# Turning roped rows one step later, and a new order of VectorE's and ScalarE's work at a head's end

## The chip, the cores and the metric

The kernel runs on one core of a Trainium2 chip. Four compute engines work side by side, each on its own list of instructions: TensorE (PE: matrix products and transposes, which write to PSUM), VectorE (DVE), ScalarE (ACT) and GpSimd (POOL). They wait for each other by semaphores. The metric is the device time of one execution in microseconds (us).

## The reference

One layer of an encoder, applied with the same weights to a prompt of 256 and a sample of 512 tokens of width 1024. In short:

```
h   = rms_norm(x)
p   = h @ w_in                         # q, k, v, gates, ... of all head groups
a   = gated linear attention (4 heads, chunks of 64, forward and backward scans summed)
d   = differential attention (4 heads, QK norm and rotary embedding)
x   = x + concat(a, d) @ w_out
x   = x + expert_choice_swiglu(rms_norm(x))   # 16 experts, each picks its own tokens
```

The change touches the place where `d`'s query and key columns are projected, normed and rotated while `a` is computed:

```
q = apply_rope(rms_norm(q, qn_g)) * (DIFF_DH ** -0.5)
k = apply_rope(rms_norm(k, kn_g))
scores = einsum('bhncd,bhnsd->bhncs', q * exp(b - b_mid), k * exp(b_mid - b))   # of the linear attention
```

## The kernel before

All 768 tokens are held as six tiles of 128. Every fp32 product is made of three: both operands are split into a high and a low part, and high x high, low x high and high x low are summed in PSUM. Weights are therefore split as they come: ScalarE writes the high part (`high_parts`, line 1017), VectorE the low part (`low_parts`, line 1375). The projection runs by slices of 512 columns of `w_in`; a slice has eight parts of 128 rows, and the buffer `wih` for high parts exists once, so the next slice's can only be written when the last product of the slice before is done.

The change lies in the head loop, 24 steps (`BODY = 4 * NT`), six to each of the four heads of the linear attention. Step i (head h = i // 6, tile t = i % 6) holds one projection unit on TensorE: 24 matmuls of 128x512 for tile t of the slice that belongs to head h. Heads 0 and 2 have the slices with the query and key columns of the differential attention (`dqk` units, "rotary" steps); heads 1 and 3 have slices that need only a copy (`tok` units). Around them, written out by hand, stands the rest:

- Rotary steps, for row number v: TensorE's product; ScalarE squares it (`squares`, line 1060); VectorE sums the squares (`sum_squares`, line 1470); ScalarE takes logarithm and exponential (`root_qk`, lines 1067 and 1068); VectorE refines them to inverse roots (`inverse_roots`, lines 1482 to 1484); ScalarE scales the rows from PSUM to `yr` (`rows_scaled`, line 1076), which frees the PSUM bank. One step later GpSimd multiplies the swapped halves (line 502), VectorE does the cosine half (`cosine_half`, line 1492) and the sum of both (`rope_add`, line 1476). TensorE turns the roped rows (a `rope` unit, line 644), two steps after their product, and ScalarE copies them out (line 1048).
- Linear attention of head h: `factors` (ScalarE's exponentials, lines 1097 to 1100, in step 3) for head h + 1; `score_factors` (VectorE, lines 1432 and 1433) multiplies them with queries and keys, and GpSimd multiplies the state keys (`state_factors`, line 514). TensorE makes `scores` (line 665) at the start of the head, VectorE masks them (`mask`, line 1443, for the prompt and for the sample), TensorE turns the keys (line 677) in the first step, does the updates (line 690) in the second and the outputs (lines 702 and 706) in the fourth.
- Last step of a head (t = 5, `turning`): high and low parts of the next slice.

Each engine takes its instructions in the order in which they are written. A unit takes the PSUM bank `u % 4`, u being its number in `tile_plan`, and waits until the unit u - 4 has been read out:

```python
if 4 <= u < len(UNITS) - 2:
    pe.wait_ge(*freed_count(u - 4))
```

`tile_plan` lists dqk, rope, gate and tok units in TensorE's order. Before, step 3 to 7 read: dqk(3), rope(1), dqk(4), rope(2), dqk(5), rope(3), tok(0), rope(4), tok(1), rope(5), where rope numbers are row numbers.

## Time and profile before

| | us |
|---|---|
| median of 3 runs | 1540.5 (1540.43 to 1540.51) |
| span of the profiled execution, first to last instruction | 1538.5 |
| TensorE busy | 1503.3 |
| VectorE busy | 1242.1 |
| ScalarE busy | 1090.5 |
| GpSimd busy | 141.4 |

The head loop takes from about 95 to 268 us of the span. The diff's other end, the expert layer, is three quarters of the whole and is not touched. Starts are counted from the span's first instruction. A duration of several pipelined instructions reaches a little past the start of the next one.

### The profile page before, as it was taken

The numbers are of one execution on the slowest core, as the hardware profiler recorded it, in microseconds if no ns is written. First come the engines' busy times: TensorE is split into PE (matmuls) and PEld (weight loads), VectorE is DVE, ScalarE is ACT, GpSimd is POOL, SyncE is SP. The second block draws the span as 40 slices with busy tenths as digits, with TensorE's granted clock in tenths as the row PEclk, the third lists the DMA queues.
The fourth block names the chain that finished last, engine by engine and source line by source line (L and its number), as shares of the span: only waits on it lengthen the run. The fifth ranks groups of instructions, "written<-read, shape, count | busy, mean of one in ns | idle before, by whom it ended". The sixth has DMA issues, their size and how long they took to land.

```text
span 1538.5 us, 18603 instructions
## 1 busy us (share of the span) xinstructions
PE 1503.3 (98%) x7293; PEld 1227.3 (80%) x7293; DVE 1242.1 (81%) x1133; ACT 1090.5 (71%) x1230; POOL 141.4 (9%) x105
## 2 busy tenths in 40 slices
PE   7999999999989999999999999999999999999997
PEld 6787777678868888888888888888888888888886
DVE  5348578785589898888889888888989888898985
ACT  7556356775447778787787778787787877778784
POOL 1023131000000101010110101011010101101010
PEclk9999999999999999999999999999999999999999
DMA  6111101401759999999999999999999999999992
GB/s 233 56 55 56 37 19 56 153 28 56 274 180 389 376 386 369 394 380 393 376 388 383 379 394 379 393 376 388 384 377 392 381 393 375 392 379 386 393 376 77
DMA packets 191942, 447.98 MB, mean 291 GB/s; under 512 B 12968, under 2 KB 13296, under 8 KB 191856
## 3 DMA queue, kind: packets, MB, share of 16 engines
q1 hardware_dynamic: 187440, 433.03, 75.5%
q0 software_dynamic: 3968, 12.65, 3.5%
q8 instruction: 58, 0.95, 0.3%
q10 hardware_dynamic: 448, 1.12, 0.2%
q14 instruction: 28, 0.23, 0.0%
HBM read 434.19 MB, written 12.58 MB: 290 GB/s over the span
## 4 chain that ended last, share of the span: by engine, by line
PE 89%; DVE 5%; ACT 3%; issue 1%; DMA 1%; POOLq 0%; POOL 0%; SPq 0%; ACTq 0%; DVEq 0%
PE ps L924 23%; PE ps L926 23%; PE ps L925 23%; PE ps L597 5%; PE ps L599 4%; PE ps L598 4%; PE ps L959 1%; PE ps L813 1%; PE ps L847 1%; DVE states L1461 1%; DVE slice_low L1375 1%; PE ps L917 1%; DMA slice_raw<-in_w_in 1%; ACT yr L1076 1%; DVE t L1492 1%
## 5 line engine op out<-in xcount | busy, mean ns | idle before, releaser
L1786 DVE TENSOR_TENSOR wl<-raw,wh 128x2048 fp32r<-128x2048 f32 x384 | 873.1, 2290 | 125.9 <-ACT wh L1310 124.3
L1310 ACT CAST wh<-raw 128x2048 fp32r<-128x2048 f32 x384 | 731.3, 1913 | 125.0 <-PE ps L926 122.8
L924 PE MATMUL ps<-wh,XTh 128*128 128x512 f32 x1024 | 404.9, 395 | 0.9 <-issue 0.9
L926 PE MATMUL ps<-wl,XTh 128*128 128x512 f32 x1024 | 399.5, 390 | 0.0
L925 PE MATMUL ps<-wh,XTl 128*128 128x512 f32 x1024 | 398.5, 389 | 0.0
L926 PEld LDWEIGHTS ps<-wl,XTh 128*128 128x128 f32 x1024 | 192.2, 188 | 41.2
L924 PEld LDWEIGHTS ps<-wh,XTh 128*128 128x128 f32 x1024 | 192.3, 188 | 38.8 <-issue 1.1
L925 PEld LDWEIGHTS ps<-wh,XTl 128*128 128x128 f32 x1024 | 192.5, 188 | 38.1
L924 PE MATMUL ps<-wh,gTh 128*128 128x512 f32 x512 | 200.9, 392 | 0.0
L926 PE MATMUL ps<-wl,gTh 128*128 128x512 f32 x512 | 199.4, 390 | 0.0
L925 PE MATMUL ps<-wh,gTl 128*128 128x512 f32 x512 | 199.2, 389 | 0.0
L926 PEld LDWEIGHTS ps<-wl,gTh 128*128 128x128 f32 x512 | 96.1, 188 | 20.3
L925 PEld LDWEIGHTS ps<-wh,gTl 128*128 128x128 f32 x512 | 96.2, 188 | 19.6
L924 PEld LDWEIGHTS ps<-wh,gTh 128*128 128x128 f32 x512 | 96.1, 188 | 19.3
L549 POOL DMA_INDIRECT y_sample<-Ys,tabf x16 | 22.9, 1429 | 923.3 <-ACT Yp L1325 815.5
L597 PE MATMUL ps<-wih,HTh 128*128 128x512 f32 x240 | 96.2, 401 | 0.8 <-DVE slice_low L1375 0.8
L599 PE MATMUL ps<-slice_low,HTh 128*128 128x512 f32 x240 | 93.8, 391 | 0.0
L598 PE MATMUL ps<-wih,HTl 128*128 128x512 f32 x240 | 93.6, 390 | 0.0
L1375 DVE SCALAR_TENSOR_TENSOR slice_low<-slice_raw,st,wih 128x512 fp32r<-128x512 f32 x48 | 34.1, 777 | 44.2 <-ACT wih L1017 44.0
L1330 ACT CAST gTh<-ps 128x384 fp32r<-128x384 f32 x64 | 30.8, 481 | 53.1 <-PE ps L959 52.7
L1351 ACT ACTIVATE hid<-ps 96x512 f32<-96x512 f32 x64 | 38.1, 596 | 35.7 <-PE ps L926 35.7
L597 PEld LDWEIGHTS ps<-wih,HTh 128*128 128x128 f32 x240 | 45.0, 188 | 15.2 <-issue 2.3
(244 smaller groups left out, 1571.1 us busy)
## 6 DMA issues: line engine op xcount, KB each, us to landing
raw<-in_w_gate SPq DMA_DIRECT2D x128, 1024.0 KB, 9.4
raw<-in_w_up SPq DMA_DIRECT2D x128, 1024.0 KB, 9.6
raw<-in_w_down SPq DMA_DIRECT2D x128, 1024.0 KB, 9.9
slice_raw<-in_w_in SPq DMA_DIRECT2D x6, 2048.0 KB, 8.1
X<-in_x_sample SPq DMA_DIRECT2D x8, 512.0 KB, 12.4
slice_raw<-in_w_out SPq DMA_DIRECT2D x2, 2048.0 KB, 9.0
X<-in_x_prompt SPq DMA_DIRECT2D x4, 512.0 KB, 4.2
h_rows<-hn SPq DMA_DIRECT2D x4, 512.0 KB, 3.3
```

The costliest lines, as they stand in the source:

```text
L549: pool.indirect_dma_start(out=y_sample[0], out_offset=bass.IndirectOffsetOnAxis(ap=sidx[0:CAP_S, e:e + 1], axis=0), in_=Ys[e % 2][0:CAP_S, ...
L597: pe.matmul(out, lh, rh, start=(k == first), stop=False)
L598: pe.matmul(out, ll, rh, start=False, stop=False)
L599: return pe.matmul(out, lh, rl, start=False, stop=(k == last))
L924: pe.matmul(out, hi, rhs_h, start=first, stop=False)
L925: pe.matmul(out, lo, rhs_h, start=False, stop=False)
L926: return pe.matmul(out, hi, rhs_l, start=False, stop=last)
L1310: act.copy(wh[:, n % CONV, :], raw[:, n % RAW, :]).then_inc(s_wh, 1)
L1330: act.copy(gTh[act_buffer(q)][:, :, 0:CAP], ps[:, 6, 0:FC * CAP].rearrange("p (f c) -> p f c", f=FC)).then_inc(s_gth, 1)
L1351: act.activation(hid[0:CAP], ps[0:CAP, TILES[n - 1][1] % 2, :], ACT.Silu).then_inc(s_silu, 1)
L1375: dve.scalar_tensor_tensor(slice_low[n % 2][:, k, :], slice_raw[n % 2][:, k, :], gcol1[:, k:k + 1], wih[:, k, :].bitcast(F32), ALU.mult, A ...
L1786: dve.tensor_tensor(wl[:, n % CONV, :], raw[:, n % RAW, :], wh[:, n % CONV, :].bitcast(F32), ALU.subtract).then_inc(s_wl, 1)
```

## The change

It does four things. A roped row is turned by TensorE three steps after its product (`ROPE_LAG`), not two, and the plan of units and the copies of ScalarE follow; this also changes which bank each unit takes. `score_factors` of the next head comes first on VectorE in step 4. In the last step of a head all eight high and all eight low parts stand at a stretch, the squares and copies of the step behind them. The two masks of the next head are done in the last step of the head, one ahead of the step's sum of squares and one behind it, and `cosine_half` comes behind `inverse_roots` in each step.

```diff
--- before.py
+++ after.py
@@ -37,6 +37,7 @@
 SLICES = (C_QK, C_V, C_DQ, C_OG, C_DK, C_DV)
 FIRST = 2
 BODY = 4 * NT
+ROPE_LAG = 3
 FILL = {1: ("unit", 4, 0), 3: ("unit", 5, 0),
         6: ("turn", 0, 0), 7: ("turn", 1, 0), 8: ("half", 0, 0), 9: ("half", 1, 0), 10: ("turn", 2, 0),
         11: ("turn", 3, 0), 12: ("half", 2, 0), 13: ("half", 3, 0), 14: ("half", 0, 1), 15: ("half", 1, 1),
@@ -83,8 +84,8 @@
     for i in range(BODY):
         h, t = i // NT, i % NT
         plan.append(("tok" if rotary(i) is None else "dqk", FIRST + h, t))
-        if rotary(i - 2) is not None:
-            plan.append(("rope", 0, rotary(i - 2)))
+        if rotary(i - ROPE_LAG) is not None:
+            plan.append(("rope", 0, rotary(i - ROPE_LAG)))
         if t == 1 and h + 1 < HEADS:
             plan += [("gate", h + 1, 0), ("gate", h + 1, 1)]
     return plan
@@ -731,8 +732,8 @@
                     scores(h, 1)
                 if i < BODY - 2:
                     unit("tok" if rotary(i) is None else "dqk", FIRST + h, t)
-                if rotary(i - 2) is not None:
-                    unit("rope", 0, rotary(i - 2))
+                if rotary(i - ROPE_LAG) is not None:
+                    unit("rope", 0, rotary(i - ROPE_LAG))
                 if t == 0:
                     turn_keys(h, 0)
                     turn_keys(h, 1)
@@ -1160,7 +1161,7 @@
                 h, t = i // NT, i % NT
                 turning = t == NT - 1 and h + 1 < HEADS
                 if turning:
-                    high_parts(FIRST + h + 1, range(0, 4))
+                    high_parts(FIRST + h + 1)
                 if rotary(i) is not None:
                     squares(i)
                 else:
@@ -1170,10 +1171,9 @@
                     if i < BODY - 2:
                         copy_unit("tok", FIRST + h, t)
                 if turning:
-                    high_parts(FIRST + h + 1, range(4, KD))
                     inter_factors(h + 1)
-                if rotary(i - 2) is not None:
-                    copy_unit("rope", 0, rotary(i - 2))
+                if rotary(i - ROPE_LAG) is not None:
+                    copy_unit("rope", 0, rotary(i - ROPE_LAG))
                 if rotary(i) is not None:
                     root_qk(rotary(i))
                 if t == 4:
@@ -1552,22 +1552,24 @@
             dve.wait_ge(s_tab, 4)
             for i in range(BODY):
                 h, t = i // NT, i % NT
-                if t == 0:
-                    mask(h, 0)
-                    mask(h, 1)
+                if i == 0:
+                    mask(0, 0)
+                    mask(0, 1)
                 v = rotary(i)
                 turning = t == NT - 1 and h + 1 < HEADS
+                if t == 4 and h + 1 < HEADS:
+                    score_factors(h + 1)
                 if turning:
-                    low_parts(FIRST + h + 1, range(0, 4))
+                    low_parts(FIRST + h + 1)
+                    mask(h + 1, 0)
                 if v is not None:
                     sum_squares(v)
                 if turning:
-                    low_parts(FIRST + h + 1, range(4, KD))
-                if rotary(i - 1) is not None:
-                    cosine_half(rotary(i - 1))
+                    mask(h + 1, 1)
                 if v is not None:
                     inverse_roots(v)
                 if rotary(i - 1) is not None:
+                    cosine_half(rotary(i - 1))
                     rope_add(rotary(i - 1))
                 if t == 1:
                     if h + 1 < HEADS:
@@ -1576,8 +1578,6 @@
                     carry(h, 1)
                 if t == 2 and h + 1 < HEADS:
                     sums(h + 1)
-                if t == 4 and h + 1 < HEADS:
-                    score_factors(h + 1)
                 if i == 3 * NT + 2:
                     dve.wait_ge(s_e3, HEADS)
                     dve.wait_ge(s_dlast, HEADS)
```

The first place is VectorE from step 4's last work in head 0 to the masks of head 1. L1432 and L1433 are the score factors, L1375 the low parts, L1470 the sum of squares, L1492 the cosine half, L1482 to L1484 the inverse roots, L1476 the rope sum and L1443 the masks. Before:

```order
L1432 TENSOR_TENSOR qtil<-qtil,Q 128x768
L1433 TENSOR_TENSOR zT_89<-zT_89,K 128x768
L1375 SCALAR_TENSOR_TENSOR slice_low_56<-slice_raw_54,st,wih 128x512 x4
L1470 TENSOR_REDUCE st<-yr_58 128x8
L1375 SCALAR_TENSOR_TENSOR slice_low_56<-slice_raw_54,st,wih 128x512 x4
L1492 TENSOR_TENSOR t_1_60<-yr_57,tabs 128x512
L1482 SCALAR_TENSOR_TENSOR st<-st 128x8
L1483 SCALAR_TENSOR_TENSOR st<-st 128x8
L1484 SCALAR_TENSOR_TENSOR st<-st 128x8
L1476 TENSOR_TENSOR t_1_60<-t_1_60,t_62 128x512
L1443 COPY_PREDICATED Ssb<-pmask,ps 128x256 x2
L1443 COPY_PREDICATED Ssb<-pmask,ps 128x512 x2
```

The changed kernel has the same from its step 4:

```order
L1432 TENSOR_TENSOR qtil<-qtil,Q 128x768
L1433 TENSOR_TENSOR zT_89<-zT_89,K 128x768
L1470 TENSOR_REDUCE st<-yr_57 128x8
L1482 SCALAR_TENSOR_TENSOR st<-st 128x8
L1483 SCALAR_TENSOR_TENSOR st<-st 128x8
L1484 SCALAR_TENSOR_TENSOR st<-st 128x8
L1492 TENSOR_TENSOR t_0_59<-yr_58,tabs 128x512
L1476 TENSOR_TENSOR t_0_59<-t_0_59,t_62 128x512
L1375 SCALAR_TENSOR_TENSOR slice_low_56<-slice_raw_54,st,wih 128x512 x8
L1443 COPY_PREDICATED Ssb<-pmask,ps 128x256 x2
L1470 TENSOR_REDUCE st<-yr_58 128x8
L1443 COPY_PREDICATED Ssb<-pmask,ps 128x512 x2
```

The score factors moved from behind step 4's rotary work to ahead of it; the low parts are one block; both masks now stand between the low parts and step 5's inverse roots.

The second place is ScalarE in the same stretch, from the scaling of step 4's rows (L1076) over the high parts (L1017), squares (L1060), the factors for the outputs (L1106 and L1107), a copy of turned rows (L1048) and the roots (L1067, L1068) to the scaling of step 5's rows. Before:

```order
L1076 ACTIVATE yr_57<-ps,st 128x64 x8
L1017 ACTIVATE wih<-slice_raw_54,st 128x512 x4
L1060 ACTIVATE yr_58<-ps 128x512
L1017 ACTIVATE wih<-slice_raw_54,st 128x512 x4
L1106 ACTIVATE qhat<-cum 128x768
L1107 ACTIVATE decay<-blast 128x12
L1048 COPY QT<-ps 128x4x128
L1067 ACTIVATE st<-st,eps 128x8
L1068 ACTIVATE st<-st 128x8
L1076 ACTIVATE yr_58<-ps,st 128x64 x8
```

The changed kernel, where each line number is one higher:

```order
L1077 ACTIVATE yr_57<-ps,st 128x64 x8
L1018 ACTIVATE wih<-slice_raw_54,st 128x512 x8
L1061 ACTIVATE yr_58<-ps 128x512
L1107 ACTIVATE qhat<-cum 128x768
L1108 ACTIVATE decay<-blast 128x12
L1049 COPY QT<-ps 128x4x128
L1068 ACTIVATE st<-st,eps 128x8
L1069 ACTIVATE st<-st 128x8
L1077 ACTIVATE yr_58<-ps,st 128x64 x8
```

The squares of step 5 moved behind the second half of the high parts.

The third place is TensorE from the end of step 6's product to the start of step 7's, with what each waits for: the turned rows, the turned keys, the product. Before:

```order
L599 MATMUL ps<-slice_low_56,HTh 128x512
L644 MATMUL ps<-ident,t_1_60 128x128 [waits roped,unit_copied_by_act]
L644 MATMUL ps<-ident,t_1_60 128x128 x3
L677 MATMUL ps<-ident,zT_90 128x128 [waits gla_masked,state_keys]
L677 MATMUL ps<-ident,zT_90 128x128 x5
L597 MATMUL ps<-wih,HTh 128x512 [waits unit_scaled_by_act]
```

The changed kernel:

```order
L600 MATMUL ps<-slice_low_56,HTh 128x512
L645 MATMUL ps<-ident,t_0_59 128x128 [waits roped,unit_copied_by_act]
L645 MATMUL ps<-ident,t_0_59 128x128 x3
L678 MATMUL ps<-ident,zT_90 128x128 [waits gla_masked,state_keys]
L678 MATMUL ps<-ident,zT_90 128x128 x5
L598 MATMUL ps<-wih,HTh 128x512 [waits unit_scaled_by_act]
```

The rows turned here are one step older (row 3, not row 4). Step 7's product (the last row) waits for the same count of scaled rows in both, that of step 5. In the plan steps 3 to 7 now read: dqk(3), rope(0), dqk(4), rope(1), dqk(5), rope(2), tok(0), rope(3), tok(1), rope(4); four places ahead of dqk(5) stands dqk(3), as before, and four ahead of tok(1) stands dqk(5), as before.

## Rows read from the trace of the kernel before

**Rows 1.** The page, its first part: busy time of the engines.
```profile
PE 1503.3 (98%) x7293; PEld 1227.3 (80%) x7293; DVE 1242.1 (81%) x1133; ACT 1090.5 (71%) x1230; POOL 141.4 (9%) x105
```

**Rows 2.** Waits of TensorE: waiter, releaser: us in total, times, longest.
```profile
PE ps L644 <- DVE t L1476: 2.8, 4, 0.7
PE ps L665 <- DVE zT L1433: 2.0, 2, 1.0
PE ps L677 <- DVE Ssb L1443: 0.7, 2, 0.3
```

**Rows 3.** Timeline, TensorE, steps 5 to 7: start, us, instruction, idle before.
```profile
133.65 0.48 PE L597 MATMUL ps<-wih,HTh 128*128 128x512 f32 x1
...
141.05 1.61 PE L665 MATMUL ps<-qtil,zT 64*128 64x128 f32 x24 [1.02 <-DVE zT L1433]
142.59 0.50 PE L597 MATMUL ps<-wih,HTh 128*128 128x512 f32 x1
...
145.99 0.47 PE L597 MATMUL ps<-wih,HTh 128*128 128x512 f32 x1 [0.24 <-DVE slice_low L1375]
...
149.67 0.63 PE L644 MATMUL ps<-ident,t 128*128 128x128 f32 x4 [0.64 <-DVE t L1476]
150.63 0.85 PE L677 MATMUL ps<-ident,zT 128*128 128x128 f32 x6 [0.33 <-DVE Ssb L1443]
151.23 0.47 PE L597 MATMUL ps<-wih,HTh 128*128 128x512 f32 x1
```

**Rows 4.** Timeline, VectorE, step 0 (first two rows), then steps 4 to 6.
```profile
102.20 0.66 DVE L1470 TENSOR_REDUCE st<-yr 128x8 f32<-128x512 f32 x1
103.47 0.17 DVE L1482 SCALAR_TENSOR_TENSOR st<-st 128x8 f32<-128x8 f32 x1 [0.61 <-ACT st L1068]
...
136.22 0.69 DVE L1470 TENSOR_REDUCE st<-yr 128x8 f32<-128x512 f32 x1 [3.90 <-ACT yr L1060]
...
141.09 3.51 DVE L1375 SCALAR_TENSOR_TENSOR slice_low<-slice_raw,st,wih 128x512 fp32r<-128x512 f32 x4
...
145.11 2.72 DVE L1375 SCALAR_TENSOR_TENSOR slice_low<-slice_raw,st,wih 128x512 fp32r<-128x512 f32 x4
147.76 0.68 DVE L1492 TENSOR_TENSOR t<-yr,tabs 128x512 f32<-128x512 f32 x1
...
149.56 2.37 DVE L1443 COPY_PREDICATED Ssb<-pmask,ps 128x256 f32<-128x256 uint32 x4
```

**Rows 5.** Timeline, ScalarE, steps 3 to 5.
```profile
131.74 1.75 ACT L1076 ACTIVATE yr<-ps,st 128x64 f32<-128x64 f32 x8 [1.22 <-DVE st L1484]
...
134.07 0.90 ACT L1098 ACTIVATE zT<-zT 128x768 f32<-128x768 f32 x1
...
138.69 1.75 ACT L1076 ACTIVATE yr<-ps,st 128x64 f32<-128x64 f32 x8 [0.46 <-DVE st L1484]
140.28 2.60 ACT L1017 ACTIVATE wih<-slice_raw,st 128x512 fp32r<-128x512 f32 x4
...
148.95 1.75 ACT L1076 ACTIVATE yr<-ps,st 128x64 f32<-128x64 f32 x8 [1.39 <-DVE st L1484]
```

**Rows 6.** Timeline, GpSimd in head 0, then VectorE and GpSimd in head 1.
```profile
135.77 1.86 POOL L514 TENSOR_TENSOR zT<-zT,K 128x768 f32<-128x768 f32 x1 [0.76 <-ACT zT L1100]
...
175.36 0.96 DVE L1432 TENSOR_TENSOR qtil<-qtil,Q 128x768 f32<-128x768 f32 x1 [1.64 <-ACT zT L1098]
...
176.14 1.89 POOL L514 TENSOR_TENSOR zT<-zT,K 128x768 f32<-128x768 f32 x1 [1.09 <-ACT zT L1100]
176.23 2.60 DVE L1433 TENSOR_TENSOR zT<-zT,K 128x768 f32<-128x768 f32 x1
```

**Rows 7.** Timeline of TensorE, start; then windows: engines busy, PEclk, DMA, GB/s.
```profile
13.69 0.36 PE L597 MATMUL ps<-HTh,wih 128*128 128x256 f32 x1 [2.71 <-DVE slice_low L1375]
...
10.00:15.00 5.00, 2.22 (x11) 1.74 (x11) 4.28 (x7) 4.14 (x7) 0.00 (x0) 0.92 1.04 406
15.00:20.00 5.00, 4.38 (x25) 4.00 (x25) 4.26 (x8) 4.94 (x11) 0.00 (x0) 0.74 1.08 370
```


## The prediction

> **What bounds the kernel now.** I read the page first: TensorE is busy for 98% of the span [rows 1], so a change pays only where TensorE stands still. The list of its waits [rows 2] shows what the changed code could touch: turned rows waiting for their sum on VectorE (4 times, 2.8 us), scores waiting for their factors (2 times, 2.0 us), turned keys waiting for the mask (2 times, 0.7 us). Then I followed one rotary head turn (steps 3 to 7, head 0) in the timeline of TensorE [rows 3]. The reader is to see five things there. Step 5's product starts at 133.65, with one of the waits for turned rows (0.7 us, behind step 3's product) in the time before it. The scores of head 1 start at 141.05 after 1.02 us of waiting. Step 6's product starts at 142.59, right behind them. Its turned rows (149.67) and the turned keys (150.63) waited 0.64 and 0.33 us. Step 7's product starts at 151.23 and waited for nothing. Head 2 has the same turn into head 3 some 93 us later. All that the change can win is thus 2.8 + 2.0 + 0.7 us and twice the 0.24 us that step 6's product waits inside for a low part (at 145.99): 6.0 us at the very most. The turn from head 1 to head 2 has no rotary rows and no such waits.
>
> **One dependence decides.** A product takes a PSUM bank that was last used by the unit four places ahead in the plan. Step 7's product takes the bank of step 5's rotary product, before and after the change, and that bank is free only when ScalarE has scaled its rows. Before, this scaling runs from 148.95 for 1.75 us, to 150.70 [rows 5]; TensorE comes at 151.23. The margin is 0.5 us. What the change does to the scaling of step 5 is therefore the question.
>
> **Turning three steps late.** The wait of 0.7 us behind step 3's product goes: the sum for row 1 is there long before the end of step 4. But in the new plan step 5's product takes the bank of step 3's product, whose rows ScalarE scales from 131.74 to 133.49 [rows 5]. TensorE, freed of the wait and of one turn of about 0.4 us, would come at 133.65 - 0.7 - 0.4, about 132.5, and waits until 133.5 or so; before it started at 133.65. So this part is worth 0.1 us, not 0.7. Moving the cosine behind the inverse roots makes each VectorE step longer by about 0.6 us where VectorE is the late one (steps 2 and 3), but takes the cosine out of the way of the inverse roots. I take these two as cancelling for step 3's scaling; the bound is 0 to +0.6 us. The waits of 0.64 us at step 6's turned rows and 0.33 us at the keys go as well: rows three steps old are ready, and the mask's first group now stands before the end of step 6's product. So far the gain is 0.1 + 0.64 + 0.33 + 0.24 us a turn, if nothing else is late.
>
> **Score factors first in step 4.** Before, they follow step 4's sum, cosine and inverse roots. Now VectorE waits for ScalarE's exponentials, which end at 134.07 + 0.90 = 134.97 [rows 5], and does both multiplications before the sum of squares. TensorE's wait of 1.02 us at the scores goes, since they are asked for at 139.5. The price lies in what is queued behind. Alone the two multiplications would take 2 x 0.96 less an overlap, 1.85 us. The same pair stands in head 1, started as here by that exponential: it begins at 175.36 and the second one, at 176.23, takes 2.60 us, because GpSimd's multiplication of the state keys started at 176.14 and ran 1.89 us; it ends at 178.83, that is 3.47 us after the first began [rows 6]. In head 0 GpSimd starts the same multiplication at 135.77 [rows 6], 0.8 us after the exponential, just as in head 1. So I take 3.47: the factors end at 138.45, and the sum of squares of step 4 starts at 138.4 in place of 136.22 [rows 4]. From a sum to the inverse roots it is 1.27 us (102.20 to 103.47 [rows 4]), and 0.6 us for these: scaling of step 4 starts at 140.3, against 138.69 before [rows 5]. That is 1.6 us later; with 1.85 us for the pair it would be 138.7, no later at all.
> The Trainium skill (SBUF — State Buffer, "Who interferes with whom") says that issue order decides which of the two engines blocks. By that rule VectorE's second multiplication would escape if it were issued before GpSimd's, and the pair would cost 1.85 us; the row in head 1 has GpSimd 0.09 us ahead, and the sum goes by the row.
>
> **All high and low parts at a stretch, the masks ahead.** ScalarE's high parts follow its scaling: they start at 140.28 + 1.6 = 141.9, and VectorE's low parts 0.8 us behind them, at 142.7 in place of 141.09 [rows 4, 5]. Eight low parts take 3.51 + 2.72 us less small overlaps, 6.1 us: to 148.8. TensorE's step 6 product, which follows them, starts at about 143.6 and ends with its turns at about 150.7. Behind the low parts VectorE now does the two masks (2.37 us as traced, 2.25 us to the next instruction [rows 4]), the sum of squares (0.6), and only then the inverse roots (0.6). ScalarE's logarithm and exponential (1.27 us from the start of the sum) hide under the second mask, which is about 1.4 of the 2.25. Before, the sum stood between the low parts, and from their end to the scaling it was 147.76 to 148.95, 1.2 us. Now: 148.8 + 2.25 + 0.6 + 0.6 = 152.2, and the scaling ends 1.75 us later, at 154.0. TensorE starts step 7's product at 154.0 instead of 151.23: **2.8 us later a turn**, with a wait of 3.3 us just ahead of it. Without the hold-up by GpSimd all times from 138.4 on are 1.6 us earlier, the start is 152.4 and the loss 1.2 us. Even then the masks alone eat the margin: 2.25 us of masks, less the 0.6 us of sum and the cosine that left, against 0.5.
> Head 1 is not rotary: VectorE and ScalarE have slack there and TensorE has no wait, so the loss is carried on in full; gates, updates and outputs shift with TensorE. The turn from head 1 to head 2 keeps its order on VectorE; only ScalarE's copy moves behind the high parts, worth 0.1 us at most. Behind the head loop TensorE is busy to the end and nothing gives the time back. Head 2's turn repeats head 0's.
>
> **The sum.** 2 x 2.8 - 0.1 = +5.5 us. The profiled execution has a span of 1538.5 us, 2.0 below the median of 1540.5; so the span becomes 1544.0 and the time **1546.0 us**.
>
> **A clock that falls** would come on top. The only trace of it: after a gap of 2.71 us ahead of 13.69 us the granted clock fell to the lower level of 1.2 GHz, and over 10 to 15 and 15 to 20 us it was 0.92 and 0.74 of full; that is 0.4 + 1.3 = 1.7 us of work lost [rows 7]. My wait of 3.3 us is longer than that gap, so it can happen at one turn (1547.7) or both (1549.4). I don't put it in the forecast because TensorE has been dense for 100 us here, unlike in the first 13.
> The Trainium skill (TensorE: Matmul & The Clock Gate, "HAM oscillation") says that idle gaps above a few microseconds bring the lower clock. By that rule the case is close to even, which the chance below reflects.
>
> **Rivals.** (1) GpSimd doesn't hold the score factors up: 2 x 1.2 - 0.1 = +2.3 us, 1542.8. For it: a shift of 0.1 us in who starts first. Against: the row in head 1. (2) The clock falls at one or both turns: 1547.7 to 1549.4. (3) Faster: step 7's bank is not late. This decides if the scaling of step 5 ends before TensorE has done its turns. Then each turn keeps 0.1 + 1.02 + 0.24 + 0.64 + 0.33, less what the low parts cost by starting late, 1.6 us or nothing: 1539 to 1536. It would need the scaling 3 us earlier than I have it, so the masks would have to be all but free; the rows give them 2.25 us. (4) The change does next to nothing, since each wait is replaced by one of equal size: 1540.5. It lies between (1) and (3).
>
> **How the numbers follow.** Forecast as worked out, clock kept: 0.45. Rival (2): 0.25. Rival (1): 0.13. Rival (4): 0.08. Rival (3): 0.07. The rest, 0.02, is above 1550. 0.2% is 3.1 us, about what a measurement of this kernel can tell from no change. Slower by more than that: 0.45 + 0.25 + 0.02 and a little of (1), 0.75. Within it: 0.17. Faster: 0.08. The range takes in (1), the forecast and (2): 1542.5 to 1549.4.
>
> **What would show it.** Right: TensorE's longest new wait, about 3.3 us, stands ahead of step 7's product and of the same place in head 2's turn, released by ScalarE's scaling; a wait of about 1 us ahead of step 5's product; the second score factor of head 0 takes 2.6 us; no waits of turned rows or scores are left. Wrong: step 7's product with no wait (the margin was larger than I read), or the second score factor at 0.96 us.

## The result and the profile after

| | median (lowest to highest), us | span of the profiled execution, us |
|---|---|---|
| before | 1540.51 (1540.43 to 1540.88) | 1538.5 |
| changed | 1547.43 (1546.54 to 1547.96) | 1546.1 |

The changed kernel takes 1.0044 of the time before (95% interval 1.0032 to 1.0056): 6.9 us slower. The profiled execution is the slowest of the four, so its span grew by a little more, 7.6 us.

The page of the changed kernel, its first part: no engine has more work of note than in [rows 1]; most of the 3 us more of TensorE's busy time are matmuls at a slower clock, below.

```profile
PE 1506.3 (97%) x7293; PEld 1231.5 (80%) x7293; DVE 1243.2 (80%) x1133; ACT 1090.0 (71%) x1230; POOL 139.1 (9%) x105
```

The list of TensorE's waits: waiter, releaser, us in total, times, longest. The three lines of [rows 2] are gone from it. Two lines for L598, the first matmul of a product's group of three, now lead it. The first is new; the second stood in the list before with 3.5 us and has grown:

```profile
PE ps L598 <- ACT yr L1077: 7.3, 4, 2.9
PE ps L598 <- DVE slice_low L1375: 7.1, 6, 2.6
```

The four waits for ScalarE's scaling are one ahead of step 5's product and one ahead of step 7's, at each of the two turns from a rotary head. The timeline of TensorE over the first turn (start, us, instruction, idle time before it and its releaser) answers to [rows 3]:

```profile
133.78 0.50 PE L598 MATMUL ps<-wih,HTh 128*128 128x512 f32 x1 [1.32 <-ACT yr L1077]
...
139.88 1.95 PE L666 MATMUL ps<-qtil,zT 64*128 64x128 f32 x24
...
143.80 0.59 PE L598 MATMUL ps<-wih,HTh 128*128 128x512 f32 x1 [1.97 <-DVE slice_low L1375]
...
150.99 0.60 PE L645 MATMUL ps<-ident,t 128*128 128x128 f32 x4
...
154.02 0.50 PE L598 MATMUL ps<-wih,HTh 128*128 128x512 f32 x1 [1.78 <-ACT yr L1077]
```

The scores (139.88), turned rows (150.99) and the turned keys behind them wait for nothing now; step 6's product waits 1.97 us for its first low part, step 7's 1.78 us for the bank. Step 7's product starts at 154.02 in place of 151.23. What delayed that bank is read on VectorE, then ScalarE, then GpSimd, in the same stretch (answering to [rows 4 to 6]):

```profile
135.23 0.96 DVE L1432 TENSOR_TENSOR qtil<-qtil,Q 128x768 f32<-128x768 f32 x1 [1.88 <-ACT zT L1099]
136.10 2.60 DVE L1433 TENSOR_TENSOR zT<-zT,K 128x768 f32<-128x768 f32 x1
138.62 0.67 DVE L1470 TENSOR_REDUCE st<-yr 128x8 f32<-128x512 f32 x1
...
142.91 5.87 DVE L1375 SCALAR_TENSOR_TENSOR slice_low<-slice_raw,st,wih 128x512 fp32r<-128x512 f32 x8 [1.03 <-ACT wih L1018]
148.80 0.94 DVE L1443 COPY_PREDICATED Ssb<-pmask,ps 128x256 f32<-128x256 uint32 x2
...
150.22 1.52 DVE L1443 COPY_PREDICATED Ssb<-pmask,ps 128x512 f32<-128x512 uint32 x2
151.65 0.14 DVE L1482 SCALAR_TENSOR_TENSOR st<-st 128x8 f32<-128x8 f32 x1
```

```profile
140.50 1.76 ACT L1077 ACTIVATE yr<-ps,st 128x64 f32<-128x64 f32 x8
...
152.23 1.75 ACT L1077 ACTIVATE yr<-ps,st 128x64 f32<-128x64 f32 x8 [1.34 <-DVE st L1484]
```

```profile
136.00 1.88 POOL L515 TENSOR_TENSOR zT<-zT,K 128x768 f32<-128x768 f32 x1 [0.77 <-ACT zT L1101]
```

GpSimd's multiplication starts 0.10 us ahead of VectorE's second score factor, and that takes 2.60 us. The sum of step 4's squares (L1470) starts at 138.62 in place of 136.22, the low parts at 142.91 in place of 141.09, and the two masks hold the inverse roots of step 5 (L1482) until 151.65. Its scaling then starts at 152.23, against 148.95 before.

To see where the loss enters and whether it is given back, I compare the starts of the same instructions in both kernels along TensorE's timeline. Before (step 8's product, head 1's outputs, the product of step 13, that of step 19, which is step 7's place in the second turn, head 3's outputs). The middle turn is the one from head 1 to head 2, the second turn that from head 2 to head 3:

```profile
160.15 0.50 PE L597 MATMUL ps<-wih,HTh 128*128 128x512 f32 x1
...
171.17 0.38 PE L702 MATMUL ps<-V,Ssb 128*128 128x128 f32 x2
...
195.14 0.48 PE L597 MATMUL ps<-wih,HTh 128*128 128x512 f32 x1
...
244.58 0.47 PE L597 MATMUL ps<-wih,HTh 128*128 128x512 f32 x1
...
263.25 0.38 PE L702 MATMUL ps<-V,Ssb 128*128 128x128 f32 x2
```

and after:

```profile
162.95 0.50 PE L598 MATMUL ps<-wih,HTh 128*128 128x512 f32 x1
...
174.44 0.38 PE L703 MATMUL ps<-V,Ssb 128*128 128x128 f32 x2
...
198.12 0.48 PE L598 MATMUL ps<-wih,HTh 128*128 128x512 f32 x1
...
250.39 0.79 PE L598 MATMUL ps<-wih,HTh 128*128 128x512 f32 x1 [2.88 <-ACT yr L1077]
...
270.88 0.38 PE L703 MATMUL ps<-V,Ssb 128*128 128x128 f32 x2
```

The lag is 2.79 us at step 7's product, 2.80 at step 8's, 3.27 at head 1's outputs, 2.98 after the middle turn, 5.81 at step 19's product and 7.63 at head 3's outputs. The span grew by 7.6, so nothing is given back behind the head loop. In pieces: 2.8 for the first turn, 0.5 between step 8's product and the outputs, -0.3 for the middle turn, 2.8 for the second turn, 1.8 behind it. The last piece holds the 0.5 again and 1.3 us of a slower clock: step 19's product takes 6.91 us to its turned rows at 257.30, step 7's takes 5.58 (154.02 to 159.60). The windows show it (busy time and count of PE, PEld, DVE, ACT, POOL, then PEclk, DMA, GB/s):

```profile
143.80:147.40 3.60, 3.60 (x9) 2.63 (x10) 3.60 (x6) 3.60 (x7) 0.45 (x1) 0.53 0.84 319
...
250.40:254.00 3.60, 3.60 (x10) 2.88 (x11) 2.29 (x2) 3.57 (x6) 3.59 (x3) 0.61 0.01 2
```

The granted clock over the first part of step 19's product is 0.61, a mixture of the upper level, 2.4 GHz, and the lower, 1.2. Over step 6's product it is 0.53. That cost nothing here: TensorE had to wait for the bank behind it anyway.

### The profile page after: what moved, and what is told of

The parts are those of the page before. It is cut to its first block, busy times and chain, and to the rows that moved or that the text cites. A ratio compares the mean times of both kernels' runs of the same rounds, so it can differ in the third digit from the quotient of the medians.

```text
span 1546.1 us, 18600 instructions
## 1 busy us (share of the span) xinstructions
PE 1506.3 (97%) x7293; PEld 1231.5 (80%) x7293; DVE 1243.2 (80%) x1133; ACT 1090.0 (71%) x1230; POOL 139.1 (9%) x105
## 4 chain that ended last, share of the span: by engine, by line
PE 90%; DVE 4%; ACT 4%; issue 1%; DMA 1%; POOLq 0%; POOL 0%; SPq 0%; ACTq 0%; DVEq 0%
PE ps L925 23%; PE ps L927 23%; PE ps L926 23%; PE ps L598 5%; PE ps L600 4%; PE ps L599 4%; PE ps L960 1%; PE ps L814 1%; PE ps L900 1%; PE ps L848 1%; DVE states L1461 1%; DVE slice_low L1375 1%; ACT yr L1077 1%; PE ps L918 1%; DMA slice_raw<-in_w_in 1%
## 5 line engine op out<-in xcount | busy, mean ns | idle before, releaser
L598 PE MATMUL ps<-wih,HTh 128*128 128x512 f32 x240 | 97.1, 404 | 11.8 <-ACT yr L1077 7.3
L1375 DVE SCALAR_TENSOR_TENSOR slice_low<-slice_raw,st,wih 128x512 fp32r<-128x512 f32 x48 | 33.3, 764 | 46.3 <-ACT wih L1018 46.3
L598 PEld LDWEIGHTS ps<-wih,HTh 128*128 128x128 f32 x240 | 45.8, 191 | 26.1 <-ACT yr L1077 8.3
```

Source lines behind the costliest of these rows:

```text
L598: pe.matmul(out, lh, rh, start=(k == first), stop=False)
L1375: dve.scalar_tensor_tensor(slice_low[n % 2][:, k, :], slice_raw[n % 2][:, k, :], gcol1[:, k:k + 1], wih[:, k, :].bitcast(F32), ALU.mult, A ...
```

## The experiments

My theory was the prediction's: the bank of step 5's product is scaled late, for two reasons of one size, the hold-up of the score factors by GpSimd (1.6 us) and the masks ahead of the inverse roots. The rivals were that the late turning itself gains or costs, that one of the two reasons does nothing, or that the wait ahead of step 7's product has another cause than the bank. Times stand against the kernel before, run beside each.

**Late turning alone.** The kernel before with

```diff
-        if rotary(i - 2) is not None:
+        if rotary(i - 3) is not None:
```

in the plan, on TensorE and in ScalarE's copies.

> The kernel before with one thing changed: roped rows are turned three steps late. Bank theory (step 7's product waits for the scaling of step 5's rows): all waits for turned rows go, a wait of about 1 us appears ahead of step 5's product, step 7's product starts at 151.2 as before, and one turn of 0.36 us is still to be done behind it: +0.7 us over two turns, 1541.2 us. Rival (each wait of TensorE that goes comes back as time): -2.7 us, 1537.8.

Measured: 1541.05 against 1540.02 us, ratio 1.0007 (0.9997 to 1.0016). TensorE, timeline:

```profile
133.43 0.50 PE L597 MATMUL ps<-wih,HTh 128*128 128x512 f32 x1 [1.07 <-ACT yr L1076]
...
150.49 0.85 PE L677 MATMUL ps<-ident,zT 128*128 128x128 f32 x6 [1.16 <-DVE Ssb L1443]
```

Worth nothing, as said: the wait for turned rows behind step 3's product turned into one of 1.07 us for the bank ahead of step 5's, and at step 6 the turned keys wait 1.16 us for their mask where before they waited 0.33 [rows 3]. The difference of 1.0 us is within the interval; 0.7 was expected, for turns of rows that are still owed. The rival that gains 2.7 us falls.

**Score factors first, alone.** The kernel before with

```diff
+                if t == 4 and h + 1 < HEADS:
+                    score_factors(h + 1)
                 if turning:
                     low_parts(FIRST + h + 1, range(0, 4))
...
-                if t == 4 and h + 1 < HEADS:
-                    score_factors(h + 1)
```

> The kernel before with one thing changed: VectorE does the next head's score factors first in step 4. Bank and hold-up theory: the second factor takes 2.6 us beside GpSimd's state keys, the sum of step 4 starts at 138.6 in place of 136.2, high and low parts start 1.7 us late, the turned rows behind step 5's product wait 1.5 us, and step 7's product starts at 152.8: 1.6 us a turn, +3.2 us, 1543.7 us. Rival (the hold-up is hidden, the loss comes from the masks and the lower clock alone): within 1 us of the kernel before.

Measured: 1542.82 against 1540.02 us, 1.0017 (1.0008 to 1.0027): +2.8, where 3.2 were expected. VectorE and TensorE:

```profile
135.82 2.60 DVE L1433 TENSOR_TENSOR zT<-zT,K 128x768 f32<-128x768 f32 x1
```

```profile
152.50 0.47 PE L597 MATMUL ps<-wih,HTh 128*128 128x512 f32 x1
```

The second factor takes 2.60 us here too, and step 7's product starts 1.27 us later than before. So this edit alone costs 2.8 us, but not through the bank: step 5's scaling ends at 151.97 and the product waits for nothing. With rows turned two steps late, the delay reaches TensorE through the rope sums (a wait of 1.61 us behind step 5's product), the low parts and the mask.

**Score factors back at the end of step 4**, in the changed kernel (the same lines moved the other way).

> The changed kernel with the score factors put back behind step 4's rope sum. Hold-up theory: both factors take 0.96 us, the sum of step 4 is back at 136.3, the scaling of step 4 at 138.6, low parts start at about 141.5, TensorE waits about 1.5 us at the scores, and step 7's product starts at 152.8 in place of 154.0: 2.4 us less than the changed kernel over two turns, with no fall of the clock 1544. Rival (the factors' place doesn't matter, the masks do it all): step 7's product at 154.0.

Measured: 1544.21 us, 1.0030 (1.0018 to 1.0043). VectorE, then TensorE:

```profile
140.45 1.48 DVE L1433 TENSOR_TENSOR zT<-zT,K 128x768 f32<-128x768 f32 x1
```

```profile
141.98 1.61 PE L666 MATMUL ps<-qtil,zT 64*128 64x128 f32 x24 [2.06 <-DVE zT L1433]
...
152.91 0.50 PE L598 MATMUL ps<-wih,HTh 128*128 128x512 f32 x1 [2.54 <-ACT yr L1077]
```

Step 7's product comes 1.1 us earlier than in the changed kernel (154.02), and the scores wait again, 2.06 us where I expected 1.5: the second factor takes 1.48 us, not the expected 0.96, since it now meets GpSimd's swapped halves. The time came out at the expected 1544: 4.2 us above the kernel before, where the changed kernel is 6.9 above. Of the difference of 2.7, 2 x 1.1 are the earlier bank. In the profiled execution the clock stayed up at both turns, which gives 1.3 us more against the profiled execution of the changed kernel; how often it fell in the others isn't known.

**Less work for GpSimd.** The changed kernel, with the state keys of the second half of the tokens not multiplied (that half is left out of the computation), so that GpSimd's multiplication is half as long:

```diff
-                pool.tensor_tensor(khat[:], khat[:], K[:, h, :], ALU.mult).then_inc(s_kh, 1)
+                pool.tensor_tensor(khat[:, 0:TOK // 2], khat[:, 0:TOK // 2], K[:, h, 0:TOK // 2], ALU.mult).then_inc(s_kh, 1)
```

> The changed kernel with GpSimd multiplying only the first half of each head's state keys (the other half is left out, so the linear attention's states are not computed in full). Hold-up theory: GpSimd's instruction takes 0.95 in place of 1.88 us, VectorE's second score factor 1.7 in place of 2.6, and everything behind it moves up by 0.9 us: step 7's product starts at 153.1, 1.8 us less than the changed kernel over two turns. Rival (VectorE's 2.6 us have another cause than GpSimd): the second factor stays at 2.6 and the time with it.

Measured: 1546.50 (1544.88 to 1549.01), 1.0039 (1.0025 to 1.0054). GpSimd, VectorE, TensorE and a window behind step 7's start:

```profile
136.01 1.06 POOL L515 TENSOR_TENSOR zT<-zT,K 128x384 f32<-128x384 f32 x1 [0.77 <-ACT zT L1101]
```

```profile
136.11 1.77 DVE L1433 TENSOR_TENSOR zT<-zT,K 128x768 f32<-128x768 f32 x1
```

```profile
153.21 0.79 PE L598 MATMUL ps<-wih,HTh 128*128 128x512 f32 x1 [2.92 <-ACT yr L1077]
```

```profile
153.00:158.00 5.00, 4.79 (x14) 3.84 (x15) 2.99 (x2) 1.88 (x5) 3.71 (x3) 0.66 0.00 0
```

VectorE's multiplication is untouched and falls from 2.60 to 1.77 us when GpSimd's falls from 1.88 to 1.06: in both kernels it ends 0.8 us behind GpSimd's. The bank comes 0.8 us earlier, as expected (0.9). The hold-up is shown by the trace and not by the time: the medians differ by 0.9 us, within the intervals, where 1.8 was expected; the lowest executions differ by 1.7. In both profiled executions the clock fell twice, once ahead of a wait for the bank, which hid it, and once where nothing hid it; here that is behind the wait of 2.92 us (0.66 over the window).

**Masks back at the start of the next head**, in the changed kernel:

```diff
+                if t == 0:
+                    mask(h, 0)
+                    mask(h, 1)
...
-                    mask(h + 1, 0)
...
-                if turning:
-                    mask(h + 1, 1)
```

> The changed kernel with the masks put back to the start of the next head, behind the last step's roots, cosine and rope sum. Bank theory: the scaling of step 5's rows starts 1.5 us earlier (at 150.7), but the turned keys now wait for the mask till 153, so step 7's product starts at 153.5 in place of 154.0: 0.5 us a turn, -1 us against the changed kernel; a wait for the mask of 1.5 us or more stands at the turned keys. Rival (the masks cost nothing where they are): no difference, and step 7's product at 154.0.

Measured: 1546.70 us, 1.0044 (1.0028 to 1.0061). ScalarE, then TensorE:

```profile
150.47 1.74 ACT L1077 ACTIVATE yr<-ps,st 128x64 f32<-128x64 f32 x8 [0.64 <-DVE st L1484]
```

```profile
152.94 0.85 PE L678 MATMUL ps<-ident,zT 128*128 128x128 f32 x6 [1.03 <-DVE Ssb L1443]
153.55 0.47 PE L598 MATMUL ps<-wih,HTh 128*128 128x512 f32 x1
```

The trace is clear: the scaling starts 1.8 us earlier, but the bank was then no longer what TensorE waited for. The turned keys wait for the mask instead, and step 7's product comes only 0.5 us earlier than in the changed kernel; at the second turn nothing is gained (20.2 us from step 17's product to step 19's in both). In time the two can't be told apart. Each of the two placements of the masks costs about the same, one through the bank and one through the keys, as long as the factors are late.

**Another bank for step 7.** The changed kernel, but the unit of step 7 and the turned rows behind it trade their banks, so that step 7's product takes one freed long before:

```diff
-            return 6 + u - (len(UNITS) - 2) if u >= len(UNITS) - 2 else u % 4
+            if u >= len(UNITS) - 2:
+                return 6 + u - (len(UNITS) - 2)
+            return SWAPPED.get(u, u) % 4
+        SWAPPED = {}
+        for h in (1, 3):
+            u = UNITS.index(("tok", FIRST + h, 1))
+            SWAPPED[u], SWAPPED[u + 1] = u + 1, u
...
-                    pe.wait_ge(*freed_count(u - 4))
+                    pe.wait_ge(*freed_count(used_before(u)))
```

`used_before(u)` is the last earlier unit with the same bank.

> The changed kernel with two neighbours in the plan trading banks: step 7's product takes the bank of the turned rows copied out long before, and the turned rows behind it take the bank of step 5's product. Nothing else moves. Bank theory: the wait for the scaling ahead of step 7's product is gone, the product starts right behind the turned keys at 152.1 in place of 154.0, and so at the second turn: 1542.7 us, about 4 us below the changed kernel, with no fall of the clock at that place. Rival (TensorE would have waited there for something else, such as the mask or the copied keys): a new wait and step 7's product near 154.0.

Measured: 1542.16 (1540.52 to 1543.18), 1.0011 (1.0001 to 1.0020). Waits and timeline of TensorE (lines are ten higher):

```profile
PE ps L608 <- ACT yr L1087: 2.7, 2, 1.3
```

```profile
151.80 0.48 PE L608 MATMUL ps<-wih,HTh 128*128 128x512 f32 x1
```

and a window over step 6's product:

```profile
142.00:147.00 5.00, 3.44 (x9) 2.43 (x10) 4.33 (x6) 5.00 (x10) 1.91 (x2) 0.69 0.92 353
```

Of the four waits for the scaling two are left, those ahead of step 5's product, and step 7's product starts at 151.80 with no wait. ScalarE and VectorE have the same work in the same order. So the wait is the bank's: 5.3 us of the 6.9 hang on it, in the profiled executions 2.2 at the first turn, 1.6 at the second, and 1.3 by the clock, which no longer meets a gap ahead of step 19's product. What is left, 1.7 us over the kernel before, is three losses less the waits that went. The turns of rows that are owed, explained below, are 0.9 us. Step 6's product starts 1.0 us later than in [rows 3], since its low parts are late. And here the fall of the clock within this product is not free, because no wait stands behind it: the product takes 7.23 us to its turned rows (143.56 to 150.79), and 7.63 at the second turn, against 6.05 where the clock stayed up (240.20 to 246.25 in the changed kernel). That is 2.8 us in all; without it this version would be about 1 us below the kernel before, by this estimate.

**A version meant to be faster, with the old and with the traded banks.** From the kernel before: late turning; in step 4 VectorE does sum, inverse roots, then score factors; in the last step of a head four low parts, sum, the rope sum of step 4, four low parts, inverse roots, masks. The lines that carry this on VectorE:

```diff
+                if turning and v is not None:
+                    rope_add(rotary(i - 2))
                 if turning:
                     low_parts(FIRST + h + 1, range(4, KD))
+                fourth = t == 4 and h + 1 < HEADS
+                if v is not None and (fourth or turning):
+                    inverse_roots(v)
+                if fourth:
+                    score_factors(h + 1)
+                if turning:
+                    mask(h + 1, 0)
+                    mask(h + 1, 1)
```

> Built from the kernel before, against the causes found: turned three steps late; in step 4 VectorE does the sum, at once the inverse roots, then the score factors and the cosine; in step 5 four low parts, the sum, step 4's rope sum, four low parts, the inverse roots, both masks, then cosine and rope sum. Theory: scaling of step 4 starts at 138.3 (before 138.7), the second factor ends at 140.0 beside no GpSimd work, the scaling of step 5 starts at 148.6 and ends at 150.3, the keys are turned at 149.5 and step 7's product starts at 150.4 (before 151.2), with one turn of 0.36 us still to be done: 1.0 us below the kernel before over two turns. Rival (the waits move elsewhere again): no gain.

> The kernel of e7_roots_first with the banks traded as in e6_bank_swapped. Bank theory: step 7's product no longer waits for the scaling and starts behind the turned keys at 150.1: 1.6 us below the kernel before over two turns, 0.6 below e7_roots_first.

Measured: 1539.53 against 1540.43 us, 0.9994 (0.9985 to 1.0004). The second of the two has the traded banks as well: 1539.49, 0.9994 (0.9985 to 1.0004). VectorE and TensorE of the first:

```profile
138.84 0.95 DVE L1433 TENSOR_TENSOR zT<-zT,K 128x768 f32<-128x768 f32 x1
```

```profile
150.37 0.50 PE L597 MATMUL ps<-wih,HTh 128*128 128x512 f32 x1
```

The inverse roots fill the time in which GpSimd multiplies, and the second factor takes 0.95 us. Step 7's product starts at 150.37 where it started at 151.23, as expected; each version's median is 0.9 us lower, which the interval can't tell from no change. The traded banks, from which I expected 0.6 us more, do nothing where the bank isn't late.

**High and low parts at a stretch, added to that.** The second version with `high_parts(FIRST + h + 1)` and `low_parts(FIRST + h + 1)` whole, and one mask ahead of the inverse roots:

> The kernel of e8_both with the high and the low parts at a stretch as in the change, and on VectorE behind them: sum of step 5, step 4's rope sum, the prompt's mask, the inverse roots, the sample's mask, then cosine and rope sum. Theory: the low parts run from 140.5 to 145.9 with no GpSimd work beside them, step 6's product starts at 141.4 and waits for none of them, the keys are turned at 148.0 right behind the mask and step 7's product starts at 148.7 (before 151.2): 2.2 us a turn after the turned rows still owed are paid, and 0.3 at the middle turn: 4.7 us below the kernel before. Step 5's scaling would end at 150.4, so with the banks of the kernel before 1.7 us of it would be lost. Rival (something else of step 5 is late): no more than e8_both, 1 us.

Measured: **1536.31 (1536.15 to 1536.92) against 1540.52 us, 0.9974 (0.9963 to 0.9985)**. It beats the kernel before by 4.2 us and the changed one by 11. VectorE, ScalarE and TensorE:

```profile
148.03 0.73 DVE L1491 SCALAR_TENSOR_TENSOR st<-st 128x8 f32<-128x8 f32 x1
```

```profile
149.20 1.75 ACT L1086 ACTIVATE yr<-ps,st 128x64 f32<-128x64 f32 x8 [2.04 <-DVE st L1493]
```

```profile
148.88 0.48 PE L607 MATMUL ps<-wih,HTh 128*128 128x512 f32 x1
```

Step 7's product starts before the scaling of step 5 does (148.88 against 149.20), which only the other bank allows; both turns gain: step 7's product is 2.35 us earlier than before, and step 19's, at 240.02, 4.56 us.

**The same without the traded banks**, to see what they are worth there:

> The kernel of e9_stretch_and_banks with the banks of the plan not traded. Bank theory: step 5's scaling runs from 149.2 to 150.95 as in e9_stretch_and_banks, step 7's product waits for it and starts at 151.0 in place of 148.9, 2.1 us a turn, so about 4 us above e9_stretch_and_banks and level with the kernel before. Rival (the gain of e9_stretch_and_banks comes from the order on VectorE alone): within 1 us of e9_stretch_and_banks.

Measured: 1543.15 (1541.53 to 1543.95) against 1540.19, 1.0016 (1.0006 to 1.0026). TensorE, and the window behind:

```profile
150.67 0.53 PE L602 MATMUL ps<-wih,HTh 128*128 128x512 f32 x1 [1.86 <-ACT yr L1081]
```

```profile
150.00:155.00 5.00, 4.33 (x12) 3.42 (x13) 3.59 (x5) 2.34 (x8) 3.26 (x3) 0.66 0.00 0
```

The same wait of 1.86 us stands at 245.61, and behind both the clock falls (0.66 in either window): step 7's product takes 7.18 us to its turned rows (150.67 to 157.85), in place of 5.58. That is 2 x (1.86 + 1.6) = 6.9 us, and the medians of the two versions differ by 6.8 (7.2, each taken against the kernel before beside it). I had expected only the waits and was 2.6 us low. The rival, that the order on VectorE alone makes the gain, falls.

**Two parts alone.** The kernel before with high and low parts at a stretch and nothing else:

```diff
-                    high_parts(FIRST + h + 1, range(0, 4))
+                    high_parts(FIRST + h + 1)
...
-                    low_parts(FIRST + h + 1, range(0, 4))
+                    low_parts(FIRST + h + 1)
```

> The kernel before with one thing changed: all high and all low parts at a stretch, the squares and the sum behind them. Theory: the 0.24 us inside step 6's product goes, the scaling of step 5 starts within 0.2 us of 148.95, and step 7's product starts at 151.2 to 151.4, since turned rows and mask stand where they stood: between -0.3 and +0.3 us. Rival (the stretch is what delays step 5's scaling): +1 us or more.

Measured: 1540.27 us, 0.9999 (0.9989 to 1.0008). Worth nothing alone: the low part no longer keeps step 6's product waiting, and the turned rows wait longer for their sum.

```profile
149.64 0.63 PE L644 MATMUL ps<-ident,t 128*128 128x128 f32 x4 [1.30 <-DVE t L1475]
```

And the kernel before with `cosine_half` behind `inverse_roots`:

> The kernel before with one thing changed: the cosine half behind the inverse roots in each step. Theory: the rope sum of step 2 comes 0.6 us later and TensorE waits 1.3 in place of 0.7 us for the turned rows behind step 3's product, but the scores then wait that much less, since their factors are held by ScalarE and GpSimd and not by the cosine: within 0.4 us of the kernel before. Rival (VectorE's steps each grow by 0.6 us and the growth reaches step 5): +1 us or more.

Measured: 1542.27 (1542.06 to 1547.65) against 1540.52, 1.0019 (1.0009 to 1.0028). This was a miss: +1.75 us where at most 0.4 were expected. TensorE, VectorE, TensorE:

```profile
123.29 0.63 PE L644 MATMUL ps<-ident,t 128*128 128x128 f32 x4 [1.52 <-DVE t L1476]
```

```profile
140.40 1.48 DVE L1433 TENSOR_TENSOR zT<-zT,K 128x768 f32<-128x768 f32 x1
```

```profile
141.94 1.61 PE L665 MATMUL ps<-qtil,zT 64*128 64x128 f32 x24 [1.42 <-DVE zT L1433]
```

The longer wait behind step 3's product, 1.52 us, is about what I had said (1.3). What failed is that the scores would wait that much less: VectorE's second factor now meets GpSimd's swapped halves and takes 1.48 us, so the scores wait 1.42 us in place of 1.02 [rows 3]. At the second turn the turned rows behind step 18's product wait 1.21 us as well (0.64 before); step 7's product is 0.6 us late and step 19's 1.7. Two of the ten executions took 1547.5 and 1547.7 us, with a mean granted clock of 0.99; the profiled one isn't among them, and their 5 us more stay unexplained. In the changed kernel late turning covers the waits for roped rows: none is left.

## Why the prediction was right, and where its sizes were off

Forecast 1546.0 us, measured 1547.4, inside the range and slower as said. By the steps:

- **Late turning gives little.** Right. In the changed kernel step 5's product starts at 133.78 (133.65 before, 133.5 expected) behind a wait of 1.32 us for the bank; alone the edit gains nothing.
- **Score factors, 3.47 us for the pair.** Right: from 135.23 to 138.70, the second one 2.60 us; scaling of step 4 at 140.50, said 140.3. The Trainium skill (SBUF — State Buffer, "Who interferes with whom") says that issue order decides who blocks; the traces agree: GpSimd is 0.09 us ahead in [rows 6] and 0.10 us in the changed kernel and in the run with less work for it, and VectorE is held up each time. The other order is shown in the last section. Rival (1) needed VectorE to be first and fell: all four second factors of the changed kernel take 2.60 us, where before two of the four took 0.95.
- **Masks ahead of the inverse roots.** Right: low parts end at 148.8 as said, the scaling starts at 152.23 (said 152.2), step 7's product at 154.02 (said 154.0). What the prediction said of the masks as a cause is true of the bank only; the run with the masks moved back shows that the keys would have been late in their place, so moving them alone wins 0.5 us at the first turn and nothing at the second.
- **A wait of 3.3 us ahead of it.** Off: 1.78 us at the first turn and 2.88 at the second. The step that failed is TensorE's end of step 6's product with its turns at 150.7; at the first turn it was 152.2, since the clock fell within that product; at the second, without a fall, it was 0.4 us later than said. The start of step 7's product does not depend on it.
- **The sum.** 2 x 2.8 held to 0.05 us. Two terms were mis-sized. First, a turn of rows (L645) is still owed at step 7: with the lag of three, the row that before was turned behind step 7's product is turned behind step 8's, so equal starts of step 7's product are not equal progress. That is 0.47 us at each of the two turns, 0.9 in all, and I had taken this turn out ahead of step 5 without paying it back; the bank swallowed what it gave there. Second, the middle turn gave 0.3 us, where I had 0.1.
- **The clock.** Rival (2) came true at one turn, for 1.3 us (estimated 1.7 from [rows 7]). Together 5.6 + 0.9 - 0.3 + 1.3 = 7.5 of the 7.6 us in the span. Without the fall the sum gives 1540.5 + 6.2 = 1546.7, about the fastest execution, 1546.54.

Still open is why the clock falls behind one gap and not behind another. In one and the same execution of the changed kernel it fell behind 1.97 us at 143.80 and stayed up behind 1.97 us at 240.20. With the score factors moved back it stayed up behind 2.54 us at both turns. No run varied the gap alone. Only one execution of each kernel has a trace, so how often the clock fell in the others is open too.

## What to carry to other kernels

When work is moved ahead on an engine to end a wait, follow what is now queued behind it down to the buffer that it frees: here the masks and the score factors stood ahead of three tiny instructions on the way to the scaling that released a PSUM bank, with 0.5 us of margin. A rotation of banks is a dependence of its own, and trading two of them can be worth as much as a reordering where the bank is what TensorE waits for (5.3 us here, 6.8 in the best version), and nothing where it isn't. And place a large VectorE multiplication so that short work with ScalarE round trips, not the multiplication, runs beside GpSimd's.

## What the runs showed of the hardware that I had not expected

- **The clock fell behind gaps shorter than that of [rows 7], within work that had been dense before them**: after 1.97 us (granted clock 0.53 over 143.80 to 147.40), and after 1.97 us at both turns of the changed kernel with another bank for step 7; after 1.86 us at both turns of the best version without its traded banks; after 2.88 and 2.92 us. With the masks moved back it fell behind 1.97 us at both turns, and with less work for GpSimd behind 1.50 us at 240.21. It fell as early as within the gap (that of 2.88 us) and as late as 1.8 us after TensorE had started again (240.21). It did not fall after 1.78 us at 154.02, after 1.97 us at 240.20, nor, with the score factors back, after 2.06, 2.09 and twice 2.54. Each fall made a product of 24 matmuls 1.1 to 1.6 us longer, nearly as much as the shorter of these waits. The Trainium skill (TensorE: Matmul & The Clock Gate, "HAM oscillation") says that idle gaps above a few microseconds bring the lower clock; the traces agree on the direction, but these gaps are shorter, and by their length alone no line can be drawn between those that did and those that didn't.
- **GpSimd's hold on VectorE scales with GpSimd's instruction**: VectorE's 128x768 multiplication of 0.95 us takes 2.60 beside one of 1.88 us, 1.77 beside one of 1.06, and 1.48 beside the swapped halves. The small ones are hit as well: a 128x8 instruction of the inverse roots, 0.17 us in [rows 4], took 0.73 at 148.03 in the best version. GpSimd's swapped halves ran beside it, from 147.33 to 148.74, and it ended at 148.76; that they held it is likely by this, and wasn't tested.

That the hold-up can go the other way is seen in the kernel before. VectorE's second score factor of head 0 starts 0.47 us ahead of GpSimd's two swapped halves and keeps its 0.95 us. They take 2.20 us, against 1.44 for the pair at 133.57; the first low parts run beside them as well:

```profile
140.05 0.95 DVE L1433 TENSOR_TENSOR zT<-zT,K 128x768 f32<-128x768 f32 x1
```

```profile
140.52 2.20 POOL L502 TENSOR_TENSOR t<-yr,tabs 128x256 f32<-128x256 f32 x2 [2.89 <-ACT yr L1076]
```
